# Feed-forward down projection: seven block products in place of eight over two thirds of its rows

## The reference, cut to what matters

```python
D_FF = (8 * D_MODEL + 3 * 256 - 1) // (3 * 256) * 256        # 2816 for D_MODEL = 1024
...
        h = rmsnorm(x, norm_ffn[layer])
        x = x + (jax.nn.silu(h @ w_ffn_gate[layer]) * (h @ w_ffn_up[layer])) @ w_ffn_down[layer]
    return rmsnorm(x, norm_final)
```

## Time and profile before

| | |
|---|---|
| median of 3 runs | 1795.23 us |
| span of the profiled execution (first to last instruction) | 1792.8 us |
| TensorE busy | 1773.5 us, 99% |
| VectorE busy | 923.6 us, 52% |
| ScalarE busy | 790.4 us, 44% |
| GpSimd busy | 637.7 us, 36% |
| feed-forward down matmuls | 528 of 9830, from 529.3 to 802.9 us |

### The profile page before, as it was taken

One profiled execution on the slowest core, in us unless ns is written; L12 is line 12 of the kernel. 1 busy time (PEld: TensorE's weight loads), 2 busy tenths in 40 slices (PEclk: granted clock), 3 DMA queues, 4 the chain that ended last, 5 costly groups with the idle time before them and its releaser, 6 DMA issues.

```text
span 1792.8 us, 24798 instructions
## 1 busy us (share of the span) xinstructions
PE 1773.5 (99%) x9830; PEld 1427.6 (80%) x9830; DVE 923.6 (52%) x2017; ACT 790.4 (44%) x1713; POOL 637.7 (36%) x390
## 2 busy tenths in 40 slices
PE   9999999999999999999999999999999999999997
PEld 6787877788888888889866798888877777887676
DVE  4558688554111101134877368764744243567764
ACT  5434455444321222243567345563355344446662
POOL 4534521154454443434312433224342324332222
PEclk9999999999999999999999999999999999999999
DMA  5322320153333332324212332213331222431212
GB/s 172 100 71 71 95 59 24 41 171 99 108 101 94 96 116 82 94 69 124 53 42 71 94 98 71 60 59 90 111 77 56 80 71 79 109 68 35 60 57 71
DMA packets 215173, 147.91 MB, mean 83 GB/s; under 512 B 51969, under 2 KB 197393, under 8 KB 215058
## 3 DMA queue, kind: packets, MB, share of 16 engines
q1 hardware_dynamic: 210736, 137.10, 27.3%
q10 hardware_dynamic: 4322, 9.24, 1.5%
HBM read 144.22 MB, written 2.10 MB: 82 GB/s over the span
## 4 chain that ended last, share of the span: by engine, by line
PE 89%; DVE 7%; ACT 3%; issue 0%; DMA 0%; POOL 0%; SPq 0%; DVEq 0%; ACTq 0%
PE PS L393 24%; PE PS L395 23%; PE PS L394 23%; PE PS L481 6%; PE PS L542 6%; PE PS L566 4%; PE PS L744 1%; DVE PS L1556 1%; ACT X L1085 1%; DVE X L1559 1%; DVE PS L1575 1%; PE PS L946 1%; PE PS L767 1%; PE PS L967 0%; DVE P L2070 0%
## 5 line engine op out<-in xcount | busy, mean ns | idle before, releaser
L2157 POOL TENSOR_TENSOR Wl<-Wr,Wh 128x1024 fp32r<-128x1024 f32 (+5 forms) x385 | 636.9, 1673 | 1121.5 <-ACT Wh L1026 1121.2
L393 PE MATMUL PS<-XTl,Wh 128*128 128x512 f32 (+1 forms) x1096 | 413.2, 377 | 1.0 <-DVE KF L1594 0.8
L395 PE MATMUL PS<-XTh,Wh 128*128 128x512 f32 (+1 forms) x1096 | 408.5, 373 | 0.0
L394 PE MATMUL PS<-XTh,Wl 128*128 128x512 f32 (+1 forms) x1096 | 408.4, 373 | 0.0
L1026 ACT CAST Wh<-Wr 128x1024 fp32r<-128x1024 f32 (+5 forms) x292 | 268.5, 938 | 185.5 <-PE PS L395 134.1
L393 PEld LDWEIGHTS PS<-XTl,Wh 128*128 128x128 f32 x1096 | 206.7, 189 | 45.5 <-issue 9.9
L395 PEld LDWEIGHTS PS<-XTh,Wh 128*128 128x128 f32 x1096 | 206.5, 188 | 36.4
L394 PEld LDWEIGHTS PS<-XTh,Wl 128*128 128x128 f32 x1096 | 206.7, 189 | 34.5
L393 PE MATMUL PS<-Wl,XTh 128*128 128x512 f32 (+2 forms) x608 | 227.4, 374 | 2.2 <-DVE XTl L1567 1.7
L395 PE MATMUL PS<-Wh,XTh 128*128 128x512 f32 (+2 forms) x608 | 224.3, 369 | 0.0
L394 PE MATMUL PS<-Wh,XTl 128*128 128x512 f32 (+2 forms) x608 | 224.1, 369 | 0.0
(11 more groups left out here) (323 smaller groups left out, 2495.0 us busy)
## 6 DMA issues: line engine op xcount, KB each, us to landing
Wr<-in_w_in SPq DMA_DIRECT2D x38, 512.0 KB, 3.8
Wr<-in_fox_w_in SPq DMA_DIRECT2D x32, 512.0 KB, 4.1
Wr<-in_w_ffn_gate SPq DMA_DIRECT2D x22, 512.0 KB, 3.9
Wr<-in_w_ffn_up SPq DMA_DIRECT2D x22, 512.0 KB, 3.9
Wr<-in_w_ffn_down SPq DMA_DIRECT2D x22, 512.0 KB, 3.6
Wr<-in_swa_w_in SPq DMA_DIRECT2D x20, 512.0 KB, 3.9
Wr<-in_mla_w_in SPq DMA_DIRECT2D x16, 512.0 KB, 4.0
Wr<-in_mla_w_out SPq DMA_DIRECT2D x16, 512.0 KB, 3.4
```

What stands on the lines that cost most here:

```text
L393: pe.matmul(o, l[0], r[1], start=start, stop=False)
L394: pe.matmul(o, l[1], r[0], start=False, stop=False)
L395: return pe.matmul(o, l[0], r[0], start=False, stop=stop)
L2157: ins = raw.tensor_tensor(l[:, cs], r[:, cs], h[:, cs].bitcast(F), sub)
```

## The change

The 22 tiles go in chunks of 8, 8 and 6. The chunk of 6 is computed as before. A chunk of 8 (c = 0 and c = 1) is four pairs of tiles, q = 0 to 3. A pair is a product of [tokens x 256] by [256 x 1024]: its hidden values split by token half and by tile (even, odd), its weights by tile (even row block, odd row block) and by column half. The function `seven` makes of the eight block products seven, by Strassen's method in Winograd's form. Every token half is 256 tokens, two token tiles, so a block product is 6 matmuls and a pair takes 42 in place of 48.

**Hidden side.** `HF` holds the two tiles of the pair, each in two token halves. VectorE makes four sums and differences of them into `SF`; ScalarE rounds 7 blocks of 256 columns to `FSh` in three instructions and VectorE subtracts for `FSl` in three.

**Weight side.** For each pair the even row block We comes through the raw ring and the odd row block Wo into a buffer `WO`. VectorE's `sums` makes, in four additions of 512 columns: the two halves of `W13` (We0+We1 and We1+Wo1), the second half of the even piece itself (We0+We1+Wo1, in place in `Wr`), and `W4` (that plus Wo0). The pieces of a pair are then We with its new half, `W13`, `WO`, and half a `W4`: 14 pieces for a chunk in place of 8. ScalarE rounds all of them. GpSimd makes the low parts but for the two `W4` pieces of a chunk, whose low parts VectorE makes (`fours`).

**Order in a chunk.** TensorE goes over q = 0 to 3 twice. The first pass has products A, B (even piece) and C, E (`W13`), 24 matmuls for each q, into eight banks. The second has A2, C2 (`WO`) and E2 (`W4`), 18 for each q, added on in the banks of A, C and E. Between the passes, ScalarE copies A to `u`, and VectorE adds B to `u` and subtracts C and E from `X`, while these banks are only half done; then it adds `u` to `X` in four instructions. Behind the second pass it adds or subtracts the same six banks.

```diff
+
+CHUNKS = ((0, 8), (8, 8), (16, 6))
...
+            FS = splits(cm, "FS", [128, 7, 4, 256])
...
+            HF, SF, U = (alloc(cm, n, [128, 4, 256]) for n in ("hf", "sf", "u"))
+            WO, W4 = alloc(cm, "WO", [128, 4, D]), alloc(cm, "W4", [128, 4, T])
+            W13 = [alloc(cm, "W13", [128, 2, T]) for _ in range(2)]
...
+        def split_ready(i):
+
+            kind, c, q = homes[i]
+            if kind in ("even", "sums"):
+                return by_dve.at("w2" if kind == "even" else "w13", c, q)
+            if kind == "odd":
+                return odd_in[q].at(c)
+            if kind == "fours":
+                return by_dve.at("w4", c, 2 * q + 1)
+            return loaded(i)
...
+                A, B, C, E = ([take(("dn", c, x, v)) for v in range(2)] for x in "ABCE")
...
+                for q in range(4):
+                    w2 = weight([(wd[:, f0 + 2 * q:f0 + 2 * q + 1, :], 0)], D, ("even", c, q))
+                    even[c, q] = w2
+                    w13 = weight(sums, D, ("sums", c, q))
+                    for bs, w, h, j, x in ((A, w2, 0, 0, "A"), (B, w2, 1, 5, "B"), (C, w13, 0, 4, "C"), (E, w13, 1, 3, "E")):
+                        for v in range(2):
+                            ins = product(bs, v, w, h, j, q, q == 0, q == 3)
+                            if q == 3:
+                                ins.then_inc(*done(psum_full, "dn", c, x, v))
+                        if h:
+                            if q < 3:
+                                ins.then_inc(*weight_used.next())
...
+                for q in range(4):
+                    wo = weight(whole, D, ("odd", c, q))
+                    if q % 2 == 0:
+                        w4 = weight(sums, D, ("fours", c, q // 2))
+                    for bs, w, h, j, x, read in ((A, wo, 0, 1, "A2", by_act.at("dn", c, "A", 1)), (C, wo, 1, 6, "C2", by_dve.at("dn", c, "C", 1)),
+                                                 (E, w4, q % 2, 2, "E2", by_dve.at("dn", c, "E", 1))):
+                        e.wait_ge(read)
+                        for v in range(2):
+                            ins = product(bs, v, w, h, j, q, False, q == 3, again=True)
+                            if q == 3:
+                                ins.then_inc(*done(psum_full, "dn", c, x, v))
+                        if h:
+                            if q < 3:
+                                ins.then_inc(*weight_used.next())
+                            used[w] = weight_used.now() if q < 3 else psum_full.now()
...
+                        if c < 2 and f0 + 3 <= f < f0 + 7:
+                            odd_loads[count[0]] = (c, f - f0 - 3, wd[:, 2 * f - f0 - 5:2 * f - f0 - 4, :])
...
-                outproj("ffn" if g == 2 else f"ffn{g}", wd[:, f0:f0 + n, :], HT[g % 2], lambda a: [by_dve.at("ht", f0 + a)], norm=g == 2)
...
+                if c < 2:
+                    seven(c, f0)
+                else:
+                    outproj("ffn", wd[:, f0:f0 + n, :], HT, lambda a: [by_dve.at("ht", f0 + a)])
...
-                    e.wait_ge(raw_in[i % RAW_SLOTS].at(i))
+                    e.wait_ge(split_ready(i))
...
-                    act.copy(Wh[i % W_SLOTS][:, 0:m], Wr[i % RAW_SLOTS][:, 0:m]).then_inc(*weight_hi.next(i))
+                    act.copy(Wh[i % W_SLOTS][:, 0:m], raw_of(i)[:, 0:m]).then_inc(*weight_hi.next(i))
...
-                f0 += n
...
+                    elif s:
+                        e.wait_ge(by_dve.at("fu", f))
+                        high(FS[0][:, 0, q, :], HF[:, 0, :], "fs_hi", c, q)
+                        high(FS[0][:, 1:3, q, :], HF[:, 2:4, :], "fs_hi", c, q)
+                        e.wait_ge(by_dve.at("sf", c, q))
+                        high(FS[0][:, 3:7, q, :], SF[:, :, :], "fs_hi", c, q)
+                if c < 2:
+                    for v in range(2):
+                        after(psum_full, "dn", c, "A", v)
+                        act.copy(U[:, 2 * v:2 * v + 2, :].rearrange("p a t -> p (a t)"), bank["dn", c, "A", v][:, :]).then_inc(*by_act.next("dn", c, "A", v))
...
+            def sums(c, q):
...
+                i = even[c, q]
+                r, o, t = raw_of(i), WO[:, q, :], W13[q % 2]
+                e.wait_ge(loaded(i), odd_in[q].at(c), by_dve.now())
+                if c or q >= 2:
+                    e.wait_ge(weight_lo.at(even[(c, q - 2) if q >= 2 else (c - 1, q + 2)] + 1))
+                ve.tensor_tensor(t[:, 0, :], r[:, HALVES[0]], r[:, HALVES[1]], add).then_inc(*by_dve.next())
+                ve.tensor_tensor(t[:, 1, :], r[:, HALVES[1]], o[:, HALVES[1]], add).then_inc(*by_dve.next("w13", c, q))
+                e.wait_ge(by_dve.now())
+                ve.tensor_tensor(r[:, HALVES[1]], t[:, 0, :], o[:, HALVES[1]], add).then_inc(*by_dve.next("w2", c, q))
+                e.wait_ge(by_dve.now())
+                ve.tensor_tensor(W4[:, q, :], r[:, HALVES[1]], o[:, HALVES[0]], add).then_inc(*by_dve.next("w4", c, q))
...
+            def fours(c, h):
+                i = homes.index(("fours", c, h)) if homes else 0
+                e.wait_ge(weight_hi.at(i))
+                low(Wl[i % W_SLOTS][:, :], raw_of(i), Wh[i % W_SLOTS][:, :], "w4_lo", c, h)
...
-                    e.wait_ge(by_act.at("fg", f), psum_full.at("fu", f))
-                    ve.tensor_tensor(HF[s][:, :], SG[s][:, :], bank["fu", f][:, :], mult).then_inc(*by_dve.next("fu", f))
-                    e.wait_ge(by_act.at("ht_hi", f))
-                    low(HT[g % 2][1][:, f - f0, :], HF[s][:, :], HT[g % 2][0][:, f - f0, :], "ht", f)
...
+                    if f == f0 + 7:
+                        sums(c, 2)
+                    if s:
+                        e.wait_ge(by_dve.now())
+                        ve.tensor_tensor(SF[:, 0:2, :], HF[:, 0:4:3, :], HF[:, 1, :].unsqueeze(1).broadcast_to([128, 2, 256]), sub).then_inc(*by_dve.next())
+                        e.wait_ge(by_dve.now())
+                        ve.scalar_tensor_tensor(SF[:, 2, :], SF[:, 1, :], -1.0, HF[:, 0, :], mult, sub).then_inc(*by_dve.next())
+                        e.wait_ge(by_dve.now())
+                        ve.scalar_tensor_tensor(SF[:, 3, :], SF[:, 2, :], -1.0, HF[:, 2, :], mult, sub).then_inc(*by_dve.next("sf", c, q))
+                        e.wait_ge(by_act.at("fs_hi", c, q))
+                        low(FS[1][:, 0, q, :], HF[:, 0, :], FS[0][:, 0, q, :], "fs", c, q)
+                        low(FS[1][:, 1:3, q, :], HF[:, 2:4, :], FS[0][:, 1:3, q, :], "fs", c, q)
+                        low(FS[1][:, 3:7, q, :], SF[:, :, :], FS[0][:, 3:7, q, :], "fs", c, q)
+                    if f == f0 + 6:
+                        sums(c, 0)
+                        sums(c, 1)
+                if c < 2:
+                    sums(c, 3)
+                    fours(c, 0)
+                    for v in range(2):
...
+                        e.wait_ge(by_act.at("dn", c, "A", v), psum_full.at("dn", c, "B", v))
+                        ve.tensor_tensor(u, u, bank["dn", c, "B", v][:, :], add).then_inc(*by_dve.next("dn", c, "B", v))
...
+                    for x in "CE":
+                        for v in range(2):
+                            e.wait_ge(psum_full.at("dn", c, x, v), by_dve.at("dn", c, "C", v) if x == "E" else by_dve.now())
+                            y = X[:, v + 2, HALVES[1]]
+                            ve.tensor_tensor(y, y, bank["dn", c, x, v][:, :], sub).then_inc(*by_dve.next("dn", c, x, v))
...
+                    e.wait_ge(by_dve.now())
+                    for v in range(2):
+                        u = U[:, 2 * v:2 * v + 2, :].rearrange("p a t -> p (a t)")
+                        y = X[:, v + 2, HALVES[0]]
+                        ve.tensor_tensor(y, y, u, add).then_inc(*by_dve.next())
+                        y = X[:, v::2, HALVES[1]]
+                        ve.tensor_tensor(y, y, u.unsqueeze(1).broadcast_to([128, 2, 512]), sub).then_inc(*by_dve.next())
+                    fours(c, 1)
+                    e.wait_ge(by_dve.now())
...
+                if homes[i][0] == "fours":
+                    continue
```

More of the change, by code:

```diff
@@ L334, in program @@
         mask_in, sink_in, bias_in = signal("mask_in", 16), signal("sink_in", 16), signal("bias_in", 16)
+        odd_in = [signal(f"odd_in{q}", 16) for q in range(4)]
         norm_in = [signal(f"norm_in{j}", 16) for j in range(2)]
@@ L384, in weight @@
                     pieces.append((srcs, srcs[0][0].shape[2] if len(srcs) == 1 else n))
+                    homes.append(home)
+                    if home[0] in ("ring", "even"):
+                        ring[i] = len(ringed)
+                        ringed.append(i)
                 return i
@@ L390, in part, with mm3 @@
                 return [t[0:p, a * n + c0:a * n + c1] for t in (Wh[i % W_SLOTS], Wl[i % W_SLOTS])]
[L392 to L395, removed]
+            def mm3(o, l, r, start, stop, again=False):
+                pe.matmul(o, l[0], r[1], start=start, stop=False, skip_group_check=again)
```

(41 more changed lines are left out.)

69 lines of the change are left out of this document (45 added, 24 removed).

## The result

The changed kernel takes 1803.81 us (median of 4 runs, 1800.26 to 1805.95) against 1795.17 us: a ratio of 1.0048, 95% interval 1.0034 to 1.0062. Timed again, unedited, in experiment 6 it took 1800.06 us (7 runs, 1797.69 to 1807.86) against 1794.43 us, 1.0036 [1.0022, 1.0050]. So it is 0.4 to 0.5% slower, near the forecast of 1802.4, and its runs scatter by 10 us in experiment 6 where those of the kernel before scatter by 3 at most. The profile is of the slowest of the first four runs, 1805.95 us.

A forecast was written before the change was run, and what follows sets the result against it. TensorE, busy 99% of the span, was taken to bound the kernel. Stalls of 9.0 us against 5.44 saved add 3.6 us per chunk, 7.2 in all: median 1795.2 becomes 1802.4 us, range 1787 to 1810.

The forecast's parts named there:

- What bounds, and what is saved: Feed-forward: TensorE bounds; 24 down matmuls fewer save 5.44 us in each chunk of 8, 10.9 us in all.
- Turns: One instruction during which the other waits: VectorE's with two SBUF inputs against GpSimd's; charged 2.26 us (GpSimd), 0.55 us (VectorE).
- The walk: Chunk timeline from zero, the product of the last but one tile: stalls 3.3, 0.7, 1.9, 0.3, 2.8 us, sum 9.0.
- A chunk +3.6 us: Each chunk of 8: stalls of 9.0 us against 5.44 us saved make it 3.6 us longer.
- the sum: Whole kernel: two chunks at 3.6 us, +7.2 us; profiled span 1792.8 to 1800.0 us, median 1795.2 to 1802.4 us.
- rival 4: Feed-forward: stalls bring 1.2 GHz for 24 matmuls behind the second `W4`, +10.9 us on top, 1813 us; chance 0.04.
- Rival 3: Between passes: GpSimd gets one more turn at 47.7, second `W4` 2.3 us later, chunk +5.9, 1807.0 us; chance 0.09.
- rival 2: Break-even: turns partly go VectorE's way, second `W4` in time, 2.8 us less per chunk; say 1796 us; chance 0.13.
- Rival 1: In a chunk: only ScalarE's order costs, one stall of 1.8 us, chunk 3.7 us shorter, 1787.9 us; chance 0.20.

The follow-up runs named there:

- experiment 1: Against the changed kernel, the four weight additions of each pair became same-size copies of one SBUF tile with an accumulated sum: 1793.74 us, 0.9994.
- experiment 2: Against the changed kernel, GpSimd made the low parts in the two chunks of 8 in two instructions of 512 columns: 1797.17 us, 1.0013.
- experiment 3: Against the changed kernel, ScalarE rounded `W13` of pair 1 before the hidden tile's parts of pair 3: 1803.71 us, 1.0048.
- experiment 8: Changed kernel with GpSimd's low parts halved, sums of pairs 0 and 2 and one rounding moved: 1789.01 us; with sums of pair 3 moved too: 1787.90 us.
- experiment 7: Kernel before, with TensorE made to wait for VectorE fills in the first two chunks: six fills 1807.82 us (1.0072), nine fills 1814.48 us (1.0112).

## Why the prediction was right

- **What bounds, and what is saved.** Right: TensorE, 9782 matmuls, 5.44 us for each chunk. No wait of TensorE in this stage is for a load.
- **Turns.** Right, for 1024 columns and the broadcast input too, and shown by experiments 1 and 2. The sums have a mean of 1.33 us (I said near 1.2) and a longest of 2.9.
- **The walk.** These are its key times, with the measured ones from the same zero in brackets: even piece of pair 1 summed at 9.75 (10.0) and its low part done at 13.25 (13.6), SF done at 17.5 (17.8), `W13` of pair 1 ready at 22.02 (23.3), pair 3's even piece at 32.82 (33.3), the first `WO` at 38.56 (39.0), the second `W4` at 52.25 (52.5). One turn went the other way: VectorE's wide low part got in before GpSimd at 19.9. Hence one pause of 4.6 us where I had 3.3, 0.7 and 1.9. All pauses of the first chunk sum to 7.0 us where I had 9.0, as TensorE's slow stretch fills what would have been a wait at pair 3. The chunk's end hangs on the second `W4` all the same. From the first to the last down matmul the chunks take 49.3 and 47.8 us (I said 47).
- **A chunk +3.6 us.** The second chunk of the profile is +4.0, the first +5.7.
- **How close the number is, is in part luck.** The span of this execution is 4.2 us above the walk's 1800.0, and 3.2 of that are falls of the clock, which the sum put at nothing. The other runs were faster, and so the median is only 1.4 us off.
- **What I undervalued is the clock**, rival 4 at 0.04. It fell behind each of the pauses of 3.1 to 7.8 us in the profiles here, and at times behind shorter ones. It was no case apart from the forecast, it came on top of it, and my price (24 slow matmuls in each chunk, +10.9) was too high: a fall of this profile cost 1.6 us. By the walk, the one behind a chunk's first pause even costs nothing in the end: at full clock TensorE would have been at pair 3 at 23.3 + 2.7 + 5.4 = 31.4 and waited for its piece until 33.3, when it is there now. Those on the path are the one behind the second pause of the first chunk and the one at 1122 us, 3.2 us together; behind the second chunk's second pause the clock stayed full.
- **Rival 3** asked whether GpSimd gets its turn ahead of the last update of `X`. It does not: it comes 0.8 us after the update began, and the low part behind it loses its turn, as in my walk. The turn that flips is that next one, and the other way: in experiment 6 VectorE wins it too, 2.2 us less. So a part of rival 2 (the second `W4` in time) occurs in single chunks. The runs reach down to 1797.7 us and up to 1807.9, and why the slowest were that slow was not profiled.
- Rival 1 is refuted as it stands by experiments 1 to 3, since the sums do take turns. A part of it is true: with the turns of the sums taken away, order and length still leave a pause of 3.1 us. Its time of 1787.9 us is reached only with the order changed and the turns halved (experiment 8).

How often each flip and fall occurs in runs without a profile stays open: only profiled executions show them.

## What to carry to other kernels

When matmuls are traded for additions, draw up which instructions of another engine the new additions lock out, before summing their lengths: here an addition that takes 0.69 us alone took up to 2.9. Five edits together (GpSimd's instruction halved, additions moved away from the busy stretch, one rounding moved up) turned a loss of 0.4 to 0.5% into a gain of 0.4% with the same arithmetic. One edit of order alone only moved the pause to the next piece. And price a pause of TensorE above its length: those of 4.2 and 7.8 us cost 2.7 and 2.0 us more than that, put into the kernel before with nothing else changed.

## What was not expected of the hardware

- The granted clock fell to half behind every pause of 3.1 to 7.8 us, in all nine profiles that have them (the changed kernel's and eight experiments'), and stayed full behind pauses of 1.4 us and less in the feed-forward. Behind the pauses of 2.4 us it fell in three cases of five. Behind one and the same pause of 1.5 us in a later layer it fell in two of twelve profiles.
- One program can have a wide spread: 1797.7 to 1807.9 us in experiment 6, against 1793.7 to 1796.7 for the kernel before. Pauses and falls alone do not make it: the two kernels of experiment 7 scatter by 3.2 and 1.8 us.
- A VectorE copy with one SBUF input and an accumulated sum takes 0.69 us for 512 columns beside a busy GpSimd, as an addition of two tiles does beside an idle one.
